# Two of the four block sums of every weight pair, third and fourth, issued by VectorE instead of GpSimd

## What is computed

```python
def _swiglu(h, w_gu, w_down):
    g, u = jnp.split(h @ w_gu, 2, axis=-1)
    return (jax.nn.silu(g) * u) @ w_down

h = h + _swiglu(_rmsnorm(h, norm_ffn[i]), ffn_w_gu[i], ffn_w_down[i])
```

## Time and profile before

| | |
|---|---|
| median of 3 runs | 1128.38 us (1128.16 to 1129.77) |
| the profiled execution | 1128.31 us |
| its span, first to last instruction | 1126.5 us |
| granted TensorE clock over the span | 0.998 |
| PE busy | 1112.7 us, 99% |
| VectorE busy | 884.2 us, 78%, 1309 instructions |
| ScalarE busy | 540.4 us, 48% |
| GpSimd busy | 596.2 us, 53%, 523 instructions |
| mean DMA rate | 87 GB/s |

### The profile page before, as it was taken

How to read it: one execution, slowest core, us unless ns; L and a number is a source line. 1 busy time by engine, 2 the same in 40 slices (tenths; PEclk the granted TensorE clock), 3 DMA queues, 4 the chain that set the end, 5 groups by cost and what they waited for, 6 DMA issues and landing times.

```text
span 1126.5 us, 18571 instructions
## 1 busy us (share of the span) xinstructions
PE 1112.7 (99%) x7114; PEld 1001.3 (89%) x7114; DVE 884.2 (78%) x1309; ACT 540.4 (48%) x1053; POOL 596.2 (53%) x523
## 2 busy tenths in 40 slices
PE   9999999999999999999999999999999999999997
PEld 8877778999988999988998888888999889999886
DVE  6688868999857999777389888769999746899654
ACT  6388834656302555411287777635555103566202
POOL 6467746687215666233156446644875217765241
PEclk9999999999999999999999999999999999999999
DMA  6411125233334333233211001134333344333321
GB/s 197 114 38 38 36 78 149 76 91 105 95 103 112 108 87 108 83 103 94 86 41 41 20 20 38 38 101 123 104 99 90 100 115 113 101 91 98 104 77 75
DMA packets 175399, 98.34 MB, mean 87 GB/s; under 512 B 7880, under 2 KB 171216, under 8 KB 175312
## 3 DMA queue, kind: packets, MB, share of 16 engines
q1 hardware_dynamic: 175296, 97.16, 30.3%
q10 hardware_dynamic: 16, 0.00, 0.0%
HBM read 94.01 MB, written 2.10 MB: 85 GB/s over the span
## 4 chain that ended last, share of the span: by engine, by line
PE 89%; DVE 6%; ACT 2%; issue 2%; POOL 0%; ACTq 0%; DVEq 0%; POOLq 0%
PE bank L1674 21%; PE bank L1678 21%; PE bank L1677 21%; PE bank L2114 14%; PE bank L2387 3%; PE bank L2406 1%; PE bank L2409 1%; PE bank L1904 1%; PE bank L1888 1%; DVE x_lo L3002 1%; DVE w_lo L3002 1%; PE bank L1919 1%; PE bank L1920 1%; PE bank L2318 1%; ACT s_a L1171 0%
## 5 line engine op out<-in xcount | busy, mean ns | idle before, releaser
L1674 PE MATMUL bank<-f_hi,w_lo 128*128 128x512 f32 (+1 forms) x363 | 139.7, 385 | 0.0
L1678 PE MATMUL bank<-f_hi,w_hi 128*128 128x512 f32 (+1 forms) x363 | 139.0, 383 | 0.0
L843 POOL TENSOR_SCALAR w_hi<-raw 128x1408 fp32r<-128x1408 f32 x32 | 44.7, 1396 | 178.1 <-PE bank L1678 150.9
L1677 PE MATMUL bank<-f_lo,w_hi 128*128 128x512 f32 (+1 forms) x363 | 138.9, 383 | 0.0
L1674 PE MATMUL bank<-x_hi,w_lo 128*128 128x256 f32 (+1 forms) x392 | 119.7, 305 | 0.0
L1678 PE MATMUL bank<-x_hi,w_hi 128*128 128x256 f32 (+1 forms) x392 | 118.8, 303 | 0.0
L1677 PE MATMUL bank<-x_lo,w_hi 128*128 128x256 f32 (+1 forms) x392 | 118.7, 303 | 0.0
L857 POOL TENSOR_TENSOR s<-raw 128x512 f32<-128x512 f32 x40 | 70.2, 1754 | 87.6 <-DMA raw<-in_ffn_w_gu 87.6
L1323 ACT ACTIVATE m_u<-bank 128x256 f32<-128x256 f32 x80 | 30.8, 385 | 135.1 <-PE bank L2114 93.8
L2114 PE MATMUL bank<-t_hi,x_lo 128*128 128x256 f32 x320 | 91.2, 285 | 1.1 <-DVE x_lo L3002 1.1
L1674 PE MATMUL bank<-t_hi,g_lo 128*128 128x256 f32 x320 | 90.7, 283 | 0.0
(11 more groups left out here) (390 smaller groups left out, 3664.5 us busy)
## 6 DMA issues: line engine op xcount, KB each, us to landing
raw<-in_ffn_w_gu SPq DMA_DIRECT2D x80, 512.0 KB, 5.2
raw<-in_ffn_w_down SPq DMA_DIRECT2D x32, 704.0 KB, 4.6
w_raw<-in_a_w_qkv SPq DMA_DIRECT2D x10, 512.0 KB, 5.1
w_raw<-in_a_w_o SPq DMA_DIRECT2D x8, 512.0 KB, 4.1
w_raw<-in_ffn_w_gu SPq DMA_DIRECT2D x8, 512.0 KB, 4.0
w_raw<-in_b_w_o SPq DMA_DIRECT2D x8, 512.0 KB, 3.7
w_raw<-in_b_w_in SPq DMA_DIRECT2D x4, 672.0 KB, 4.0
w_raw<-in_b_w_uq SPq DMA_DIRECT2D x4, 576.0 KB, 4.0
```

The source lines that it names most:

```text
L843: pool.tensor_scalar(w_hi[m % 2][:, 0:cols], raw_slot[r % 2][:, 0:cols], 1.0, 1.0, ALU.mult, ALU.mult) \
L1674: first = pe.matmul(o, ll, rh, start=start, stop=False)
L1677: pe.matmul(o, lh, rl, start=False, stop=False)
L1678: return pe.matmul(o, lh, rh, start=False, stop=stop)
```

## The change

GpSimd no longer issues `more_sums`. VectorE issues the same two operations on the same operands (`last_sum`), with the same semaphores and the same waits. In the steady run of units they stand in its queue between G and I, for unit j + 1; call them H1 (s2) and H2 (s4). For unit 2 they stand between `hidden(layer, 0)` and `group_lo(layer, 2, 1)`; for unit 3 ahead of `late_gate(layer, 2)`; for unit 11 ahead of the last `add_down` of half 0. GpSimd is left with s3 and s1 of every unit.

```diff
-            def more_sums(layer, j):
-
-                u, r = unit_of(layer, j), raw_unit(layer, j)
-                a12, a22 = (raw_slot[r % 2][:, i * QUART:(i + 1) * QUART] for i in (1, 3))
-                s3, s2 = (s_pair[u % 2][:, i * QUART:(i + 1) * QUART] for i in range(2))
-                pool.wait_ge(s3_ready, u + 1)
-                pool.tensor_tensor(s2, s3, a22, ALU.subtract).then_inc(s2_ready, 1)
-                pool.wait_ge(s2_ready, u + 1)
-                if j == 2:
-                    pool.wait_ge(t_ready, 4 * layer + HK)
-                elif u > 1:
-                    pool.wait_ge(g_ready, 4 * (u - 2) + 4)
-                pool.tensor_tensor(s_last[:, u % 2 * QUART:(u % 2 + 1) * QUART], a12, s2, ALU.add).then_inc(s4_ready, 1)
...
                     sums(layer, 2)
-                    more_sums(layer, 2)
                     sums(layer, 3)
                 else:
                     sums(layer, j0)
-                    more_sums(layer, j0)
                     sums(layer, j0 + 1)
                 for j in range(j0 if half else 2, j1):
-                    if j + 1 < j1:
-                        more_sums(layer, j + 1)
                     if j + 2 < j1:
                         sums(layer, j + 2)
...
+            def last_sum(layer, j):
+
+                u, r = unit_of(layer, j), raw_unit(layer, j)
+                s3, s2 = (s_pair[u % 2][:, i * QUART:(i + 1) * QUART] for i in range(2))
+                dve.wait_ge(s3_ready, u + 1)
+                dve.tensor_tensor(s2, s3, raw_slot[r % 2][:, 3 * QUART:4 * QUART], ALU.subtract).then_inc(s2_ready, 1)
+                dve.wait_ge(s2_ready, u + 1)
+                if j == 2:
+                    dve.wait_ge(t_ready, 4 * layer + HK)
+                elif u > 1:
+                    dve.wait_ge(g_ready, 4 * (u - 2) + 4)
+                dve.tensor_tensor(s_last[:, u % 2 * QUART:(u % 2 + 1) * QUART], raw_slot[r % 2][:, QUART:2 * QUART],
+                                  s_pair[u % 2][:, QUART:2 * QUART], ALU.add).then_inc(s4_ready, 1)
...
                     hidden(layer, 0)
+                    last_sum(layer, 2)
                     group_lo(layer, 2, 1)
...
                     group_lo(layer, 3, 1)
+                    last_sum(layer, 3)
                     late_gate(layer, 2)
...
                         group_lo(layer, j + 1, 1)
+                        last_sum(layer, j + 1)
...
                         group_lo(layer, HALF, 1)
+                        last_sum(layer, HALF)
                     add_down(m, b + 1, h_fin[:, m % 2, :] if final else None)
```

## The result

The changed kernel takes 1140.51 us (median of 5 runs, 1139.53 to 1141.12), the kernel before 1128.16 us on the same chip (5 runs, 1127.61 to 1129.77): the ratio on record is 1.0103, 95% interval 1.0092 to 1.0114. It is slower by 1.0%, and the two medians are 12.4 us apart (1.0109). The profiled execution took 1141.12 us, of which the span is 1139.3; the granted clock is 0.998, as before.

A forecast was written before the change was run, and what follows sets the result against it. PE, busy 99% of the span, was taken as the bound. Per layer 4.0 (start) + 2.6 + 2.5 (drift) = 9.1, less 1.5 already lost, 7.6; two layers 15.2 us, giving 1143.5 us, range 1132.5 to 1151.

The forecast's parts named there:

- G: VectorE's 128x1024 g_lo instruction in each unit, 1.21 us unheld; forecast to wait about 0.9 us for s3.
- the drift: Steady units: VectorE at 10.5 us against PE's 10.08, 0.45 a unit; 2.6 us in half 0, 2.5 in half 1.
- the start: Units 2 and 3 of each layer: three PE waits, 1.2 + 1.4 + 1.4 = 4.0 us.
- what PE had lost before: Units of the kernel before, above PE's own pace: 1.5 us a layer, 3.0 in all, subtracted from the loss.
- The unit without the lock: VectorE's own work in one unit without waits for GpSimd: 7.2 us before, 8.5 with the two added sums.
- The lock: VectorE instructions with two SBUF inputs and GpSimd sums take turns; up to 1.10 us a sum, 0 to 2.2 a unit.
- The pattern: Steady units: later VectorE work delays the next load, so s3 keeps its place; 10.5 us, or 10.7 if s3 lands later.
- The two waits in t_last: Layer start: unit 3's s3 and s1 hold two short VectorE instructions, 1.0 + 1.1 = 2.1 us.
- The signs: Expected in the later profile: x_lo heading PE's waits with ten us or more, busy times, lengths of halves and instructions.
- Relief: Rival, every unit: fewer GpSimd sums hold the lock less, 2.6 + 1.3 for 5.1 us; 1126 to 1128.5 us, chance 0.09.
- The start alone: Rival: s3 lands earlier, units take 10.1 us, no drift; 2.5 us a layer left, 1133.3 us, chance 0.15.
- Every sum held in full: Rival: both sums wait fully, 10.7 us a unit from the first; 11.1 us a layer, 1150.5 us, chance 0.10.

The follow-up runs named there:

- the third experiment: Changed kernel, but GpSimd starts s3 and s1 of a unit only once VectorE has done s4 of the one before: 1129.17 us, ratio 1.0008.

## Why the prediction was right, point by point

**The total.** 1143.5 us forecast, 1140.5 measured, slower as forecast. The mechanism was right in both of its parts, the drift and the start. The 3.0 us between the two are: the start priced 0.7 us too high, what PE had lost before 1.1 us too low, 0.8 us from the first 17 us, which wasn't forecast, and 0.6 by which the profiled execution is above the median; the drift, 0.2 too low in all, goes the other way.

**The unit without the lock: right.** 8.5 us was worked out. Taking the waits off each kernel's unit gives 10.55 - 2.02 = 8.53 in the kernel after, 9.98 - 1.46 = 8.52 with the sums moved, and 9.89 - 1.33 = 8.56 with all sums on VectorE. The kernel after has such a unit itself: ahead of the last unit of each half no sums are left for GpSimd, and VectorE goes from B to B in 8.52 us, all four times. In layer 0, half 0:

```profile
288.07 1.22 DVE L2984 TENSOR_TENSOR x_lo<-s,x_hi 128x1024 fp32r<-128x1024 f32 x1
...
296.59 1.22 DVE L2984 TENSOR_TENSOR x_lo<-s,x_hi 128x1024 fp32r<-128x1024 f32 x1
```

**The lock: right where it decides.** G 0.93 and H1 1.09 us against 0.9 and 1.1, in the place named; unit 10.55 against 10.5. The page of the Trainium skill that the prediction weighed (SBUF — State Buffer, Who interferes with whom) calls it an exclusive lock and says, of VectorE's two-port modes, that it is held for the whole instruction while the other side blocks. The rows agree, if the wait is counted from where the VectorE instruction begins. At 262.36 there were 1.22 us left of s1's record and 1.09 were lost; at 260.29, 1.07 left of s3's and 0.93 lost; in t_last 1.24 and 1.11, then 1.11 and 0.98. Each time the loss is the rest of the sum's record less 0.13 to 0.14 us. So 1.1 was the right price for a sum that has just begun, and the 11.1 us that the prediction got with 1.28 in its place was too high: the longest of those units takes 10.69.

**The pattern: partly luck.** "The pattern holds itself" is not so. In the 26 units above s3 starts 5.6 to 6.6 us after the issue of its load, and in 10 of them that moved both sums to H1 and H2, the case priced at 10.7. It takes 10.60 (waits of 1.09 and 0.98), and so the choice between the two cases, on which 1143.5 or 1150.5 was to hang, hardly mattered.

**The drift: right.** 2.46 and 2.69 us in half 1 (2.5 forecast). In half 0 the six units behind unit 3 take 2.6 us more than PE's pace in both layers (2.6 forecast).

**The start: right in kind, too large.** PE comes to unit 2 0.9 us late, unit 2 takes 11.53 us (1.45 above PE's pace) and unit 3 11.38 (1.30): 3.6 us against 1.2 + 1.4 + 1.4 = 4.0, and 3.7 in layer 1. The two waits in t_last are as priced: from its first instruction to group 0 of unit 2 it is 206.46 - 202.78 = 3.68 us after and 205.65 - 204.00 = 1.65 before, 2.03 more (2.1). What I hadn't counted is a wait that goes away further up the same queue. Kernel before, VectorE and GpSimd:

```profile
196.78 0.58 DVE L2686 TENSOR_TENSOR ms_n<-ms_n,rs_n 128x8 f32<-128x8 f32 x1
```

```profile
195.07 2.27 POOL L867 TENSOR_TENSOR s<-s,raw 128x512 f32<-128x512 f32 x1
```

and kernel after:

```profile
195.98 0.17 DVE L2668 TENSOR_TENSOR ms_n<-ms_n,rs_n 128x8 f32<-128x8 f32 x1
```

s2 of unit 2 used to end at 197.34 on GpSimd and held a tiny instruction until then, 0.58 us for 0.17. With it gone VectorE is 0.4 us earlier at all that follows, against PE too: 1.2 - 0.4 = 0.8 for product 1, and 0.89 was measured.

**What PE had lost already: misread.** I took 1.5 us a layer off, from the row at 470.60 in the earlier trace rows as the last of half 1. It isn't. The kernel before, PE:

```profile
471.32 0.28 PE L2114 MATMUL bank<-t_hi,x_hi 128*128 128x256 f32 x1
471.44 0.40 PE L1674 MATMUL bank<-f_hi,w_lo 128*128 128x512 f32 x1
```

The half ends at 471.44, at 111.72 us and not 111.00, so the excess was 1.38 + 0.84 = 2.2 us in layer 0, and 1.9 in layer 1, 4.1 in all instead of 3.0. That also lifts what the change could have given back. The sum with measured terms: 3.6 + 2.6 + 2.5 = 8.7 and 3.7 + 2.6 + 2.7 = 9.0, 17.7 in all, less 4.1: 13.6. The 0.8 us from before the units leaves 12.8, by which the two profiled executions differ. This is an account of the trace and no further test.

**The 0.8 us: open.** The row of `q_lo` on VectorE starts at 17.61 us in the kernel before and at 16.81 after, where neither has come to a changed line. In the nine traces, alike up to there, it starts anywhere between 16.79 and 17.61. So nothing shows that the change won it, and no run here finds its cause.

**The signs.** Half 0 97.0 (97 to 99), half 1 113.3 and 113.6 (113 to 114), product 3 at 212.1 (near 213), H1 at 1.78 us where GpSimd is beside it (1.7 to 1.8), GpSimd 452 busy (458): as said. G was put at 1.7 to 1.8 as well, against the prediction's own sum (1.21 + 0.9); it took 2.15. Two more failed. `x_lo` heads PE's waits, but with 4.1 us and not ten: 0.45 us a unit arrives as delays within products too short for a row of their own, and PE's busy time went up by 6.3 us (1112.7 to 1119.0) instead. And VectorE's busy time rose by 29 us, not by 54 (20 more or less): waits for the lock are counted as busy, and I had left them alike in that figure. By the groups of the timeline, kernel before:

```profile
L3002 DVE TENSOR_TENSOR x_lo<-s,x_hi 128x1024 fp32r<-128x1024 f32 x40 | 66.2, 1654 | 0.0
```

and kernel after (total us, mean ns):

```profile
L2984 DVE TENSOR_TENSOR g_lo<-raw,g_hi 128x1024 fp32r<-128x1024 f32 x40 | 69.4, 1735 | 9.3 <-ACT g_hi L1296 9.3
L2991 DVE TENSOR_TENSOR s<-s,raw 128x512 f32<-128x512 f32 x40 | 63.5, 1587 | 0.0
...
L2984 DVE TENSOR_TENSOR x_lo<-s,x_hi 128x1024 fp32r<-128x1024 f32 x40 | 48.7, 1219 | 0.0
L2997 DVE TENSOR_TENSOR s_last<-raw,s 128x512 f32<-128x512 f32 x40 | 37.5, 938 | 1.4
```

B lost its waits altogether (1654 to 1219 ns, alone 1.21 us) and they turned up in H1 (1587 for 690) and H2 (938). Added over all forms, the waits in a unit were 2.25 us for four sums and 1.7 for two. Halving the sums took off a quarter of the waiting.

**The rivals.** Relief fell: it counted the lock by the time that GpSimd holds it, and what VectorE pays goes by which of its instructions comes next. The start alone is near what the third experiment makes: s3 at another place, 9.98 us a unit, no drift, and the start as the only loss. It came out at 1129.2 and not at 1133.3, since the third piece of the start went with the drift (2.6 us a layer were left, not 4.0), and what PE had lost before was more than 1.5. Its unit, s3 in F's place and 10.1 us, stands in the trace too, at 10.13, once in each layer. Every sum held in full is what 10 of 26 units do; from the first unit on and at 10.7 us it wasn't.

## What to carry to other kernels

When two engines exclude each other, price a sum not by its length but by the instruction that the other engine has next in its queue, and compute the unit of the slower one against the pace of the engine that bounds: here a unit of 10.55 against 10.08 us cost 10.4 us of drift, and 9.98 cost none. A partial move can be worse than none or all; try the whole move, and try moving only the moment (one wait on GpSimd gave back 11 of the 12 us). Read the end of a stretch off the first row of the next one, and read the idle gaps and not the busy share, since waits for the lock are in the busy time.

## What the runs showed of the hardware

A wait for nearly a whole GpSimd sum costs a VectorE instruction with both inputs in SBUF 1.0 to 1.1 us in the rows shown (1.53 for 0.42, 1.40 for 0.42, 1.50 for 0.43, 1.78 for 0.69), whatever its own length; where an instruction that reads PSUM is ahead of it, 0.39 and 0.93 were left. In each of these rows the wait ends 0.13 to 0.14 us before the sum's record does. So short instructions suffer most by proportion: a 0.43 us one took 1.50. And GpSimd pays as well: s1 took 2.15 us beside G and 1.36 beside A. What I had not expected is that fewer sums wait dearer: 0.56 us a sum with four in a unit, 0.87 with two, since nearly all that remained met G, H1 or H2 head on.
